# A third of the convolution's taps beside the prompt attention, moved from the vector engine to the pool engine

## What is computed

```python
def gdn_features(qkv_ext, b, a, p):
    t = qkv_ext.shape[1] - (CONV_W - 1)
    w = p['gdn_conv_w']
    conv = sum(qkv_ext[:, i:i + t] * w[i] for i in range(CONV_W))
    conv = jax.nn.silu(conv.astype(F32))
    ...

def mla_prompt_attention(q_nope, q_pe, c, k_pe, p):
    ...
        s = mla_scores(qn, qp, k_nope, k_pe)
        s = jnp.where(key_pos[None, :] <= q_pos[:, None], s, -jnp.inf)
        pr = jax.nn.softmax(s, axis=-1).astype(v.dtype)
        return jnp.einsum('bhqk,bkhd->bqhd', pr, v)
```

## Time and profile before

| what | value |
|---|---|
| time, median of 3 runs | 1740.01 us (1734.2 to 1742.57) |
| the profiled execution's own time | 1740.14 us |
| its span in the trace | 1738.3 us |
| PE busy over the span | 89% |
| DVE busy over the span | 46% |
| ACT busy over the span | 36% |
| POOL busy over the span | 7% |
| prompt attention block | about 270.2 to 331.5 us |
| L948 in it (DVE, 128x512) | 36 instructions, median 744 ns |

### The profile page before, as it was taken

How to read it: one execution, slowest core, us unless ns; L and a number is a source line. 1 busy time by engine, 2 the same in 40 slices (tenths; PEclk the granted TensorE clock), 3 DMA queues, 4 the chain that set the end, 5 groups by cost and what they waited for, 6 DMA issues and landing times. The chain is left out here.

```text
span 1738.3 us, 29779 instructions
## 1 busy us (share of the span) xinstructions
PE 1546.8 (89%) x10156; PEld 1194.9 (69%) x10156; DVE 807.6 (46%) x1632; ACT 618.7 (36%) x1602; POOL 118.1 (7%) x213
## 2 busy tenths in 40 slices
PE   2999677629999999999999969999788999998999
PEld 1599534417877777777778746434434999998998
DVE  2311477765656465555557540433565222224221
ACT  3022233544555455455455430000214333334121
POOL 0000000021202021120202020000000000000000
PEclk8999886869999999999999987999899999999999
DMA  7022000022313132221313009045003332331331
GB/s 243 1 73 72 16 0 1 11 61 62 93 50 96 48 84 59 66 72 53 89 51 92 16 1 321 0 145 197 21 1 99 97 92 79 95 97 41 90 109 51
DMA packets 190602, 127.94 MB, mean 74 GB/s; under 512 B 49240, under 2 KB 176081, under 8 KB 190468
## 3 DMA queue, kind: packets, MB, share of 16 engines
q1 hardware_dynamic: 190476, 126.38, 24.9%
HBM read 120.05 MB, written 6.37 MB: 73 GB/s over the span
## 5 line engine op out<-in xcount | busy, mean ns | idle before, releaser
L1420 PE MATMUL bank<-keys_high,turned 128*128 128x512 f32 x1024 | 357.7, 409 | 7.8 <-issue 5.7
L1602 ACT ACTIVATE arena<-bank 128x512 f32<-128x512 f32 x256 | 153.2, 599 | 264.3 <-PE bank L1420 264.1
L1420 PEld LDWEIGHTS bank<-keys_high,turned 128*128 128x128 f32 x1024 | 193.1, 189 | 60.5 <-issue 13.5
L1828 DVE TENSOR_TENSOR turned<-bank,turned 128x256 fp32r<-128x256 f32 x258 | 109.4, 424 | 233.6 <-ACT turned L1595 233.1
L1420 PE MATMUL bank<-keys_low,turned 128*128 128x512 f32 x512 | 202.6, 396 | 0.0
L1834 DVE TENSOR_REDUCE arena<-arena 128x4 f32<-128x512 f32 x256 | 173.1, 676 | 0.0
L2436 PE MATMUL bank<-h_high,ffn_high 128*128 128x260 f32 x704 | 142.5, 284 | 3.0 <-DVE h_low L2494 3.0
L2436 PE MATMUL bank<-h_low,ffn_high 128*128 128x260 f32 x704 | 142.8, 284 | 0.0
L2436 PE MATMUL bank<-h_high,ffn_low 128*128 128x260 f32 x704 | 142.1, 284 | 0.0
L1910 PE MATMUL bank<-arena,yT 128*128 128x512 f32 (+1 forms) x240 | 121.4, 643 | 2.7 <-DMA arena<-in_w_mix_out 2.3
L2436 PEld LDWEIGHTS bank<-h_high,ffn_high 128*128 128x128 f32 x704 | 109.4, 190 | 3.1 <-issue 3.1
(11 more groups left out here) (460 smaller groups left out, 2622.8 us busy)
## 6 DMA issues: line engine op xcount, KB each, us to landing
arena<-in_cache_mla_ckv SPq DMA_DIRECT2D x256, 128.0 KB, 2.0
arena<-in_ffn_w_gate SPq DMA_DIRECT2D x22, 512.0 KB, 4.0
arena<-in_ffn_w_up SPq DMA_DIRECT2D x22, 512.0 KB, 5.1
arena<-in_ffn_w_down SPq DMA_DIRECT2D x16, 704.0 KB, 4.7
arena<-in_w_in SPq DMA_DIRECT2D x16, 512.0 KB, 3.8
arena<-in_cache_mla_kpe SPq DMA_DIRECT2D x256, 32.0 KB, 1.8
arena<-in_x_prompt SPq DMA_DIRECT2D x8, 512.0 KB, 6.5
arena<-in_w_mix_out SPq DMA_DIRECT2D x2, 2048.0 KB, 10.0
```

The lines of the kernel that those rows point to most:

```text
L1420: last = nc.tensor.matmul(bank[2 + n % 2][:], t[:, (2 * part + k) * P:(2 * part + k + 1) * P], w[wpart][:, k, :], start=(m == 0), stop=(m ...
L1602: nc.scalar.activation(square[n % 2], keys[:], ACT.Square)
L1828: nc.vector.tensor_tensor(t[:, KL:2 * KL], bank[n % 2][:, 0:KL], t[:, 0:KL].bitcast(F32), ALU.subtract).then_inc(p_e, 1)
```

## The change

The taps 1 to 3 of the tiles 8 to 11 leave DVE's list. `CONV_STEPS` keeps 24 entries (tiles 0 to 7), and since ceil(24 / 18) is still 2, DVE does them in turns 0 to 11 and none in turns 12 to 17. The 12 others, `POOL_STEPS`, are done by a new POOL stream in the same block. POOL gets no fused instruction for this, so each is two: a product of the shifted tile with the broadcast weight column into one of two scratch rows, and a sum into cv. The product waits for the sum two steps back, the sum waits for its own product, and at tap 1 for ACT's tap 0 of its tile. DVE's last action of turn 17 now waits for all 24 POOL instructions too.

```diff
+                @block.gpsimd
+                def _(pool):
+                    beside.pool_steps(pool)
...
-    CONV_STEPS = [(c + d, t) for c in range(0, NCC, 2) for t in range(1, TAPS) for d in range(2)]
+    POOL_C = 8
+    CONV_STEPS = [(c + d, t) for c in range(0, POOL_C, 2) for t in range(1, TAPS) for d in range(2)]
+    POOL_STEPS = [(c + d, t) for c in range(POOL_C, NCC, 2) for t in range(1, TAPS) for d in range(2)]
+    conv_pool = sem("conv_pool")
...
+        @staticmethod
+        def pool_steps(pool):
+            pool.wait_ge(conv_chain, 1)
+            for m, (c, t) in enumerate(POOL_STEPS):
+                tap = at(8704 + 512 * (m % 2), T)
+                if m >= 2:
+                    pool.wait_ge(conv_pool, 2 * m - 2)
+                nc.gpsimd.tensor_tensor(tap, qkv[:, c, t:t + T], cw[:, t, c:c + 1].broadcast_to([P, T]), ALU.mult).then_inc(conv_pool, 1)
+                if t == 1:
+                    pool.wait_ge(conv_first, c + 1)
+                pool.wait_ge(conv_pool, 2 * m + 1)
+                nc.gpsimd.tensor_tensor(cv[:, c, :], cv[:, c, :], tap, ALU.add).then_inc(conv_pool, 1)
...
             if n == of - 1:
                 dve.wait_ge(conv_chain, len(CONV_STEPS) + 1)
+                dve.wait_ge(conv_pool, 2 * len(POOL_STEPS))
                 dve.sem_inc(conv_done, 1)
```

## The result

The changed kernel takes 1745.65 us (median of 12 runs), the kernel before 1737.38 us (median of 12): the ratio is 1.0046, 95% interval 1.0027 to 1.0065. It is slower, by about 8 us, and the sign was forecast, but not the size: I had said 17 us with a range from 1742 to 1770. The time lies inside the range, near its lower end, and the change is less than half of the 17 us.

What follows compares the result with a forecast made beforehand. DVE's convolution was taken to bound turns 4 to 11 and the last three, PE mostly turns 12 to 14. Waits 19.5 + clock 2.5 - gain 4.5 = +17.5 us on 1740.14; 1757 stated, range 1742 to 1770.

Steps and rivals of the forecast that it cites:

- What is taken away: Twelve taps leave DVE's turns 12 to 17: 1.1 us in 12 to 14, 2.64 in 15 and 16, 0.75 in 17; 4.5 gained.
- POOL's prices and chain: Sums 1.286 us, products 1.031; chain from 285.5 us, 26.8 us unhindered, expected at work for 32 to 40 us.
- The wait in turn 17: DVE's new wait for POOL before its last copy: costs nothing as long as POOL takes less than 45 us.
- the cover of POOL's time: POOL's first product, at about 273 us, costs nothing, hidden by 12 us of waiting for tap 0 of tile 8.
- three instructions of a turn stand back: In each DVE turn beside POOL, both taps (L948) and the norming (L906) wait while a POOL instruction runs.
- How often DVE gets in: DVE beside POOL's stream: once per product-and-sum pair, giving +19.5 us, or after every instruction, giving +17.3 us.
- once per pair of 2.32 us: Paired case: three entries per DVE turn each wait 2.32 us; turns of 8.35 us against 3.29, +19.5 us.
- The row that misled me: L1283 in the next block, 0.18 us by its neighbour, waited through four small POOL memsets; read as back-to-back instructions not separated.
- The alternating case: DVE enters after every POOL instruction: waits of 1.0 us, turns of 6.0 us, +17.3 us; whole +15.3 us, 1755.
- +16 us: Figure named for DVE slipping in after every POOL instruction under the port-pair lock, the alternating sum.
- The clock's +2.5 us: PE at 1.2 GHz until POOL is through and into turns 9 and 10: one and a half turns at +1.7 us.
- the two cases that carried the forecast: Paired (1757) and alternating (1755) waits of DVE for POOL; together chance 0.73.

Runs made afterwards that it cites:

- the run without POOL: Changed kernel without POOL's stream and DVE's wait for it, the twelve taps left out, DVE keeping its 24: 0.9972 of the kernel before, block 55.7 us.
- the first trace: First profiled execution of the changed kernel, against the kernel before: 1745.60 us against 1740.14, block 68.95 us against 59.76.
- the second execution: The changed kernel profiled once more, unaltered, to see how much its block varies: block 68.4 us.

## Why the prediction was wrong in size

- **What is taken away** was right: 4.5 us forecast; -1.05 and -3.35 in the run without POOL, -4.6 with it from turn 11 on.
- **POOL's prices and chain** were right: sums of 1.26 and products of 1.03 us where nothing held them up. The chain began at 285.7 us and ended at 317.3, 31.6 us, where 32 to 40 were forecast. The wait in turn 17 cost nothing. One thing was missed: in the first trace the product of turn 0 met the first tap, 1.87 us for the pair in place of 1.42, some 0.5 us that I had put at nothing because POOL had time; the cover of POOL's time did not protect DVE's.
- **That three instructions of a turn stand back** was right, and is now shown: both taps and the norming are stretched in each of the turns 5 to 9, taps with one SBUF operand are not, and the loss goes with the number of POOL instructions.
- **How often DVE gets in is the step that failed.** I took "once per pair of 2.32 us", from one row of four short memsets. The turns 5 to 9 of the trace each show DVE entering between a sum and the product right behind it. Turns of 8.35 us were forecast, 5.50 came; +19.5 us were forecast for the waits, +12.2 measured (in the table's +13.4, 1.2 is PE's in turn 10). The row that misled me was one of memsets of 0.2 us. The Trainium skill, "SBUF — State Buffer", section "Who interferes with whom", has the port pair held for one whole instruction, and for these products and sums the trace agrees: DVE goes in when one of them ends.
- **The alternating case was mis-sized too**, 6.0 us a turn and +17.3. I had put each of the three waits at 1.0 us; in turn 6 they are 1.40 for the two taps together and 0.81 for the norming. And I let DVE's turn and POOL's row drift against each other, 3.6 instructions a turn, where the two lock to four in 5.50 us. The "+16 us" that the prediction names for this case beside the lock is neither of its own figures, 17.3 for the waits and 15.3 for the whole.
- **The clock's +2.5 us was too much, and the kernel before has such a term too.** In the changed kernel PE's work at 1.2 GHz fits inside DVE's turns: in the second execution it was busy for 4.89 and 4.82 of 6 us at that level and the turns stayed at 5.5 us. The first trace paid 1.2 us, in turn 10, where the level had risen near 302 us and come back to half near 308.5, PE having done nothing from 307 to 309. It is the kernel before, with turns of 3.2 us, that pays more where the level rises late: 59.8 and 62.3 us for its block. So the difference of the two blocks was 9.2 us in one pair of executions and 6.1 in the other, around the 8 us of the medians.

With 12.2 for the waits, 1.2 for the clock, 0.5 for the first product and the forecast -4.5 the sum is +9.4 us, where the block of that execution gave +9.2. That the time came within the stated range is owed to its width: the two cases that carried the forecast, 1755 and 1757, are both 9 us or more above the 1745.65 measured.

## What to carry to other kernels

Before work goes to an idle POOL, list the VectorE instructions beside it that read two SBUF operands or run `tensor_scalar` from SBUF to SBUF. Here each of the first kind waited for the product or sum in progress (not for memsets), each of the second for any POOL instruction in progress, and POOL needed two instructions for one fused tap. Ask where on the old engine's list the work disappears: here it left turns in which PE or the chain was the bound, and POOL's beginning fell into those where DVE was. Where two engines exclude each other in a loop, draw one period of both and look for the pattern that repeats, before multiplying a mean wait.

## What the hardware showed that was not expected

- A POOL that only writes (memsets of 0.96 us) left taps with two SBUF operands at 0.745 us, while products and sums stretched a pair from 1.41 to 2.4 to 3.1 us.
- DVE gets in between two POOL instructions issued without a wait if they are about 1 us long (product 1.49 in place of 1.03 us), but was once passed over by eight memsets of 128x128 in a row, 0.2 us each and 0.15 us apart (1.34 us in place of 0.42). The cause is open.
- The place where PE's clock rises in this block differs from run to run of the same kernel before (at the end of turn 7, not in turn 8 as the prediction has it, and in turn 9), and the later rise goes with 2.5 us more for its block. The changed kernel's block took 69.0 and 68.4 us, with the level back for good near 318.8 and 314.5 us.
